# Three weight blocks of the second mixer's compressed columns, cut as two halves of 336 columns

## The chip, the core and the metric

The kernel runs on one core of a Trainium2 chip. The metric is the device time of one launch in microseconds (us), lower is better. Three runs of the kernel before gave 1083.59, 1084.34 and 1084.42 us; their median is 1084.34 us.

## The reference, cut to what matters

The reference applies two transformer-like blocks to one sequence of 256 tokens with 1024 features, in float32. The change touches only the beginning of the second block, where the normalised input is multiplied by the first weight matrix, and there only the columns of the compressed query, the compressed key/value and the shared rotary part: 384 + 256 + 32 = 672 columns.

```
h = rms_norm(x, g_norm)                     # x: 256 tokens x 1024
proj = h @ w_in                             # among others 384 + 256 + 32 columns:
... c_q, c_kv, k_rope ...
q  = rms_norm(c_q, g_cq) @ w_uq             # 384 -> 768
kv = rms_norm(c_kv, g_ckv) @ w_ukv          # 256 -> 1024
k  = concatenate([k_nope, broadcast(k_rope)])
```

## The kernel before, in words

**Precision and products.** Every float32 operand of a big product is split into a rounded high part and a remainder, the low part. One product of two tiles is three matmuls: high by high, high by low, low by high (`product`, lines 523 to 527, and `first_half`, lines 530 to 539, which does the same for the first tile of a block and can make its first matmuls a few columns wider, by the table `WIDER`).

**The weight stream.** All weights come in 171 blocks of 128 x 2048 values (1 MB) in a fixed order (`weight_blocks`, `BLOCKS`, `FIRST`). SyncE loads them into a ring of three raw buffers. ScalarE rounds a block into its high part (`round_block`, line 1373), VectorE subtracts to get the low part (`low_block`, line 2091), and TensorE multiplies. There are three buffers for each of the parts, so ScalarE may round block b + 3 only when TensorE has finished block b: it waits for the counter `block_done`. `after(b)` on ScalarE and `low_after(b)` on VectorE mean "round, or lower, all blocks up to b + 3 that are not done yet". Their places in each engine's program are written out by hand, and every engine works through its program strictly in order, so an instruction behind `after(b)` cannot start before block b is finished on TensorE.

**PSUM banks.** Results go to eight banks. `claim` makes TensorE wait until the last user of a bank has read it (`bank_read`). Blocks usually take bank b modulo 3; the transposes of x take banks 3 to 6.

**The stage of the change.** After the last feed-forward part x is complete. TensorE first transposes raw x (`raw_turn(5)`); ScalarE and VectorE turn that into `sec_hi` and `sec_lo`, which are x times the gain, without the root of the norm. With tokens as the stationary side, three blocks (stages `cq`, `ckv`, `cq_rope`) are then multiplied: 256 columns, 256 columns, and 128 + 32 columns. Each has 2 token tiles x 8 k tiles x 3 = 48 matmuls. Meanwhile VectorE computes the root of the norm and scales x into `sec_xn` (lines 2136 to 2147, semaphore `xn_ready`). Between the second and the third of these blocks TensorE transposes `sec_xn` (`norm_turn(6)`, 16 transposes, line 624); from them ScalarE makes `hT_hi` (`norm_high(6)`, line 1412) and VectorE `hT_lo` (`norm_low(6)`, line 2168), which the next blocks `zz0` to `zz3` use as the moving side. `zz0` waits for its first pair of columns of `hT` only, then for each later pair as it comes to it (`ready=norm_done(6)`).

ScalarE's order here is: wait for `xn_ready` 3, scale `cq0` out of its bank (line 1892), `after` the first block, scale `ckv` out, `after` the second block, `norm_high(6)`, scale `cq1` out, then four sums of squares (lines 1916, 1919), `after` the third block, then the `zz` blocks. VectorE's order is: `norm_low(5)`, weights, sum of squares, root, scale of x (line 2147), weights of the first `zz` block, `norm_low(6)`, weights, then two roots of ten linked steps each for `c_q` and `c_kv` (`inverse_root`, lines 2121 to 2132), four scalings (`c_ready`), weights, and so on. TensorE transposes the scaled `cq` and `ckv` after `zz2` and needs `c_ready` 4 for it.

Of the kernel before, what the change touches and what calls it, by code (L numbers as in the profile page):

```python
# [15 lines left out]
P = 128  # L16
# [53 lines left out]

def weight_blocks():
# [31 lines left out]
    add("cq", "w_in_2", [(W_IN2_AT["cq"], 256)])  # L103
    add("ckv", "w_in_2", [(W_IN2_AT["ckv"], 256)])
    add("cq_rope", "w_in_2", [(W_IN2_AT["cq"] + 256, P), (W_IN2_AT["rope"], QK_ROPE)])
# [55 lines left out]
for _name, _len in [("ssd_dt_bias", 32), ("ssd_A_log", 32), ("ssd_D", 32), ("da_lambda_q1", 64), ("da_lambda_k1", 64),  # L161
# [19 lines left out]
         **dict.fromkeys(("qkv7", "qkv3", "ssd7", "kv3", "kv6", "cq0", "gg2"), (4, 4)),  # L181
         **dict.fromkeys(("gate6", "hy4"), (8, 8)),
         **dict.fromkeys(("xo2", "qkv10", "z3"), (6, 0)),
         "ckv": (4, 0), "qkv9": (2, 0), "qkv8": (12, 0), "z1": (10, 0), "out2": (12, 0)}
# [71 lines left out]
def program(nc, a, out):  # L256
    with ExitStack() as ctx:
# [242 lines left out]
        def _(pe):  # L500
# [639 lines left out]
            at = (0, 1, 2, 7, (FIRST["cq"] + 1) % 3, (FIRST["cq"] + 2) % 3)  # L1140
# [5 lines left out]
            token_block("cq0", FIRST["cq"], 256, sec_hi, sec_lo, ready=norm_done(5))  # L1146
            token_block("ckv", FIRST["ckv"], 256, sec_hi, sec_lo)
            norm_turn(6, sec_xn, 2)
            token_block("cq1", FIRST["cq_rope"], P + QK_ROPE, sec_hi, sec_lo)
            for i in range(4):  # L1150
                feature_block(f"zz{i}", FIRST["z_hy"] + i, 2, hT_hi, hT_lo, ready=None if i else norm_done(6))
                if i == 2:

                    pe.wait_ge(S("c_ready"), 4)
                    for k in range(5):
                        if k % 2 == 0:
                            o = claim(f"cT{k // 2}", 3 + k // 2)
                        for t in range(TOK):
                            src = cq[:, t, k * P:(k + 1) * P] if k < 3 else ckv[:, t, (k - 3) * P:(k - 2) * P]
                            mm = turn(o[:, k % 2 * SEQ + t * P:k % 2 * SEQ + (t + 1) * P], src)  # L1160
                        if k % 2 or k == 4:
                            ends(mm, f"cT{k // 2}")
# [199 lines left out]
        def _(act):  # L1362
# [526 lines left out]
            def token_scale(dst, src):  # L1889

                for t in range(TOK):
                    ins = act.activation(dst[:, t], src[:, t], ACT.Copy, scale=xr[:, t:t + 1])
                return ins

            o = full(act, "cq0")
            act.wait_ge(S("xn_ready"), 3)
            read(token_scale(cq[:, :, 0:256], two(o)), "cq0")
            after(FIRST["cq"])
            o = full(act, "ckv")
            read(token_scale(ckv, two(o)), "ckv")  # L1900
            after(FIRST["ckv"])
            norm_high(6, "g_norm_2", hT_hi)
            act.dma_start(dft_b[:].rearrange("p w s -> p (w s)"), a["c_dft"][:, 1024:1536]).then_inc(S("dft_ab_in"), 16)
            o = full(act, "cq1")
            token_scale(cq[:, :, 256:384], two(o)[:, :, 0:P]).then_inc(S("cq1_in"), 1)
            read(token_scale(k_rope, two(o)[:, :, P:P + QK_ROPE]), "cq1")

            for t in range(TOK):
                if t == 0:

                    wait_read(act, "cq0")
                    wait_read(act, "ckv")
                    act.wait_ge(S("cq1_in"), 1)
                else:
                    act.wait_ge(S("c_ssq"), 2)
# [5 lines left out]
            after(FIRST["cq_rope"])  # L1921
# [148 lines left out]
        def _(dve):  # L2070
# [45 lines left out]
            def inverse_root(dst, sums, n, width, eps, eps_tile=None):  # L2116
# [3 lines left out]
                if eps_tile is None:  # L2120
# [618 lines left out]
            low_after(FIRST["cq"])  # L2739
            norm_low(6, "g_norm_2", hT_hi, hT_lo)  # L2740
            low_after(FIRST["ckv"])
# [3 lines left out]
            inverse_root(rstd[:, 4:6], c_ssq[:, 0, :], 2, Q_LORA, EPS)  # L2745
            inverse_root(rstd[:, 6:8], c_ssq[:, 1, :], 2, KV_LORA, EPS)
# [17 lines left out]
            wait_read(dve, "cq1")  # L2764
# [343 lines left out]
```

## Time and profile before

| | |
|---|---|
| median of three runs | 1084.34 us |
| the profiled execution's own time | 1085.08 us |
| its span, from the first to the last instruction | 1083.2 us |
| TensorE matmul busy | 1075.2 us (99%), 8588 matmuls |
| VectorE busy | 794.2 us (73%) |
| ScalarE busy | 591.9 us (55%) |
| weights and inputs moved by DMA | 190.73 MB, mean 176 GB/s |

Matmuls are pipelined: a row's duration contains the time in flight, so two matmuls that follow each other overlap in the rows. What one costs is read from the distance between the starts of neighbours. PE is TensorE, PEld its weight load, ACT ScalarE, DVE VectorE, SP SyncE. The stage of the change lies between 866 and 885 us of the span.

### The profile page before, as it was taken

How to read it: one execution, taken by the hardware profiler on the slowest of the kernel's cores; microseconds unless marked ns; L12 is line 12 of the kernel's file. 1: busy time of each engine (PE TensorE's matmuls, PEld its weight loads, DVE VectorE, ACT ScalarE, POOL GpSimd, SP SyncE). 2: the span in 40 equal slices, each digit the busy share in tenths (PEclk: the TensorE clock that was granted, in tenths of full speed). 3: DMA queues.
4: the chain of work that ended last, by engine and by line, in shares of the span. 5: the costliest groups of instructions: out<-in, count | busy, mean ns of one | idle time of the engine just before them, and what ended most of it. 6: DMA issues, size and time to landing. Idle time of an engine off the chain costs nothing.

```text
span 1083.2 us, 21122 instructions
## 1 busy us (share of the span) xinstructions
PE 1075.2 (99%) x8588; PEld 1018.8 (94%) x8588; DVE 794.2 (73%) x1117; ACT 591.9 (55%) x842; POOL 0.2 (0%) x4
## 2 busy tenths in 40 slices
PE   9999999999999999999999999999999999999998
PEld 7999999999989999999999998999999799999998
DVE  5665657989999877778778555765655887997784
ACT  5544444578643345878445556444444575655561
POOL 0000000000000000000000000000000000000000
PEclk9999999999999999999999999999999999999999
DMA  9765556455443454444546533465555355543341
GB/s 347 285 221 205 184 182 213 151 203 186 165 156 118 137 194 157 156 160 152 205 167 242 197 109 127 145 231 196 192 182 207 117 177 204 186 156 117 118 155 40
DMA packets 29298, 190.73 MB, mean 176 GB/s; under 512 B 3656, under 2 KB 4521, under 8 KB 7466
## 3 DMA queue, kind: packets, MB, share of 16 engines
q1 hardware_dynamic: 26480, 182.53, 48.4%
q10 hardware_dynamic: 2746, 7.16, 1.9%
q8 instruction: 55, 0.90, 0.3%
q14 instruction: 17, 0.14, 0.0%
HBM read 188.62 MB, written 1.05 MB: 175 GB/s over the span
## 4 chain that ended last, share of the span: by engine, by line
PE 97%; ACT 1%; DVE 1%; DMA 0%; issue 0%; SPq 0%; ACTq 0%; DVEq 0%
PE bank L525 17%; PE bank L526 17%; PE bank L527 17%; PE bank L537 12%; PE bank L538 11%; PE bank L539 11%; PE bank L624 3%; PE bank L760 1%; PE bank L708 1%; PE bank L874 1%; PE bank L1245 1%; PE bank L1037 1%; PE bank L1081 1%; PE bank L1103 1%; PE bank L1210 1%; PE bank L1268 1%
## 5 line engine op out<-in xcount | busy, mean ns | idle before, releaser
L2091 DVE TENSOR_TENSOR sb_w_lo<-sb_w_raw,sb_w_hi 128x2048 fp32r<-128x2048 f32 x169 | 386.5, 2289 | 129.6 <-ACT sb_w_hi L1373 128.9
L1373 ACT ACTIVATE sb_w_hi<-sb_w_raw 128x2048 fp32r<-128x2048 f32 x169 | 322.8, 1910 | 31.4 <-PE bank L527 28.0
L525 PE MATMUL bank<-sb_hT_hi,sb_w_hi 128*128 128x256 f32 (+1 forms) x816 | 225.9, 277 | 0.0
L527 PE MATMUL bank<-sb_hT_hi,sb_w_lo 128*128 128x256 f32 (+1 forms) x816 | 225.9, 277 | 0.0
L526 PE MATMUL bank<-sb_hT_lo,sb_w_hi 128*128 128x256 f32 (+1 forms) x816 | 225.7, 277 | 0.0
L537 PE MATMUL bank<-sb_hT_hi,sb_w_hi 128*128 128x256 f32 (+2 forms) x744 | 213.2, 287 | 0.2 <-DVE sb_hT_lo L2168 0.2
L538 PE MATMUL bank<-sb_hT_lo,sb_w_hi 128*128 128x256 f32 (+2 forms) x744 | 206.3, 277 | 0.0
L539 PE MATMUL bank<-sb_hT_hi,sb_w_lo 128*128 128x256 f32 x744 | 206.1, 277 | 0.0
L526 PEld LDWEIGHTS bank<-sb_hT_lo,sb_w_hi 128*128 128x128 f32 (+1 forms) x816 | 152.8, 187 | 0.0
L527 PEld LDWEIGHTS bank<-sb_hT_hi,sb_w_lo 128*128 128x128 f32 (+1 forms) x816 | 152.7, 187 | 0.0
L525 PEld LDWEIGHTS bank<-sb_hT_hi,sb_w_hi 128*128 128x128 f32 (+1 forms) x816 | 152.6, 187 | 0.0
L537 PEld LDWEIGHTS bank<-sb_hT_hi,sb_w_hi 128*128 128x128 f32 x744 | 140.0, 188 | 3.8 <-issue 2.6
L538 PEld LDWEIGHTS bank<-sb_hT_lo,sb_w_hi 128*128 128x128 f32 x744 | 140.1, 188 | 1.5 <-issue 1.2
L539 PEld LDWEIGHTS bank<-sb_hT_hi,sb_w_lo 128*128 128x128 f32 x744 | 139.9, 188 | 0.0
L1427 ACT ACTIVATE sb_ffn_gate<-sb_ffn_gate 128x256 f32<-128x256 f32 x44 | 18.4, 418 | 133.2 <-DVE sb_ffn_gate L2228 133.2
L525 PE MATMUL bank<-sb_w_hi,sb_ffn_hi 128*128 128x512 f32 x156 | 60.9, 390 | 0.0
L526 PE MATMUL bank<-sb_w_lo,sb_ffn_hi 128*128 128x512 f32 x156 | 60.8, 390 | 0.0
L527 PE MATMUL bank<-sb_w_hi,sb_ffn_lo 128*128 128x512 f32 x156 | 60.8, 390 | 0.0
L1436 ACT ACTIVATE sb_ffn_hi<-sb_ffn_act 128x256 fp32r<-128x256 f32 x44 | 18.3, 416 | 48.0 <-PE bank L760 35.0
L526 PE MATMUL bank<-sb_w_lo,sb_hT_hi 128*128 128x256 f32 (+1 forms) x136 | 39.9, 293 | 0.0
L527 PE MATMUL bank<-sb_w_hi,sb_hT_lo 128*128 128x256 f32 (+1 forms) x136 | 39.9, 293 | 0.0
L525 PE MATMUL bank<-sb_w_hi,sb_hT_hi 128*128 128x256 f32 (+1 forms) x136 | 39.9, 293 | 0.0
(513 smaller groups left out, 2088.0 us busy)
## 6 DMA issues: line engine op xcount, KB each, us to landing
sb_w_raw<-in_w SPq DMA_DIRECT2D x169, 1024.0 KB, 4.9
sb_w_raw<-in_w SPq DMA_DIRECT2D x4, 512.0 KB, 7.6
sb_hT<-in_xT SPq DMA_DIRECT2D x2, 512.0 KB, 5.3
sb_x<-in_x SPq DMA_DIRECT2D x2, 512.0 KB, 11.5
sb_mem_xn<-in_mem ACTq DMA_DIRECT2D x1, 1024.0 KB, 7.3
sb_mem_T<-in_memT ACTq DMA_DIRECT2D x1, 1024.0 KB, 10.6
sb_post_g<-in_ffn_post_g ACTq DMA_DIRECT2D x2, 512.0 KB, 5.7
sb_decay<-in_c_decay ACTq DMA_DIRECT2D x1, 768.0 KB, 5.6
```

The source lines that it names most:

```text
L525: pe.matmul(o, a_hi, b_hi, start=first, stop=False)
L526: pe.matmul(o, a_hi, b_lo, start=False, stop=False)
L527: return pe.matmul(o, a_lo, b_hi, start=False, stop=last)
L537: pe.matmul(o[:, 0:width + more[0]], stat_hi, moving(move_hi, width + more[0]), start=k == 0, stop=False)
L538: pe.matmul(o[:, 0:width + more[1]], stat_hi, moving(move_lo, width + more[1]), start=False, stop=False)
L539: return pe.matmul(o[:, 0:width], stat_lo, moving(move_hi, width), start=False, stop=k == kt - 1)
L624: return pe.transpose(o, src, ident)
L708: mm = pe.matmul(o[:, i * SEQ:(i + 1) * SEQ], w[:, k, i * P:(i + 1) * P], hT[:, k, :], start=False, stop=k == KD - 1 and i == 1)
L1373: act.activation(w_hi[b % STAGES][:], w_raw[b % RING][:], ACT.Copy).then_inc(w_hi_in, 1)
L1427: act.activation(f["gate"][:, j % 2, :], f["gate"][:, j % 2, :], ACT.Silu).then_inc(S("ffn_gate"), 1)
L1436: act.activation(f["hi"][:, j % 2, :], f["act"][:, j % 2, :], ACT.Copy).then_inc(S("ffn_hi"), 1)
L2091: tt(w_lo[b % STAGES][:], w_raw[b % RING][:], f32(w_hi[b % STAGES][:]), ALU.subtract).then_inc(w_lo_in, 1)
```

## The change

The three blocks now hold two halves of 336 columns each, one after the other. Half 0 is the columns 0 to 335 of the compressed query, half 1 its last 48 columns, the 256 of the key/value and the 32 rotary ones. The first block holds the k tiles 0 to 5 of half 0; the second the k tiles 6 and 7 of half 0 and 0 to 3 of half 1; the third the k tiles 4 to 7 of half 1. A matmul is 336 columns wide, and there are 2 x 2 x 8 x 3 = 96 of them in place of 144. Each half and token tile has a bank of its own: the first two count as full when the second block is done, the other two when the third is.

The transposes `norm_turn(6)` stand inside the second block, behind the first token tile of half 1. `zz0` takes bank 6 in place of bank b modulo 3; bank 6 is also the one from which the last pair of `norm_low(6)` is read. On ScalarE `after` the first and `after` the second block come first, then `norm_high(6)`, then the four banks are scaled out. On VectorE the two roots are one of eleven linked steps over four values. The extra widths of `cq0` and `ckv` are gone.

```diff
@@ -66,6 +66,10 @@

 W_IN2_AT = {"hy": 0, "z_hy": 1536, "cq": 2048, "ckv": 2432, "rope": 2688, "z_at": 2720, "gate": 3232}
+
+
+C_WIDTH = Q_LORA + KV_LORA + QK_ROPE
+C_PARTS = (((0, 0, 6),), ((0, 6, 2), (1, 0, 4)), ((1, 4, 4),))


 def weight_blocks():
@@ -100,9 +104,8 @@
     plain("xa_q", "xa_w_q", 0, 4)
     plain("xa_o", "xa_w_o", 0, 4)
     ffn(2)
-    add("cq", "w_in_2", [(W_IN2_AT["cq"], 256)])
-    add("ckv", "w_in_2", [(W_IN2_AT["ckv"], 256)])
-    add("cq_rope", "w_in_2", [(W_IN2_AT["cq"] + 256, P), (W_IN2_AT["rope"], QK_ROPE)])
+    for part in C_PARTS:
+        add("c", "w_in_2", part)
     plain("z_hy", "w_in_2", W_IN2_AT["z_hy"], 2)
     plain("z_at", "w_in_2", W_IN2_AT["z_at"], 2)
     add("uq", "w_uq_2", [(0, 512)], 3)
@@ -178,10 +181,10 @@

 WIDER = {**dict.fromkeys(("xbc1", "xbc10", "xbc11", "qkv1", "gate0", "gate2", "gate3", "gate4", "ssd5", "attn3.0", "zz3", "gg6",
                           "gg7", "hyo1.0", "qkv2", "qkv4", "qkv5", "hy0", "gg0", "gg3", "zz1"), (2, 2)),
-         **dict.fromkeys(("qkv7", "qkv3", "ssd7", "kv3", "kv6", "cq0", "gg2"), (4, 4)),
+         **dict.fromkeys(("qkv7", "qkv3", "ssd7", "kv3", "kv6", "gg2"), (4, 4)),
          **dict.fromkeys(("gate6", "hy4"), (8, 8)),
          **dict.fromkeys(("xo2", "qkv10", "z3"), (6, 0)),
-         "ckv": (4, 0), "qkv9": (2, 0), "qkv8": (12, 0), "z1": (10, 0), "out2": (12, 0)}
+         "qkv9": (2, 0), "qkv8": (12, 0), "z1": (10, 0), "out2": (12, 0)}

@@ -1137,18 +1140,42 @@
             for i in (6, 7):
                 filter_taps(i, (up + 2) % 3 if i == 6 else (up + 1) % 3)
             ffn_part(2, 4)
-            at = (0, 1, 2, 7, (FIRST["cq"] + 1) % 3, (FIRST["cq"] + 2) % 3)
+            at = (0, 1, 2, 7, (FIRST["c"] + 1) % 3, (FIRST["c"] + 2) % 3)
             for i in range(6):
                 filter_spectrum(i, at[i])
             raw_turn(5, x_added(3))
             for i in (6, 7):
                 filter_spectrum(i, at[i - 2])
-            token_block("cq0", FIRST["cq"], 256, sec_hi, sec_lo, ready=norm_done(5))
-            token_block("ckv", FIRST["ckv"], 256, sec_hi, sec_lo)
-            norm_turn(6, sec_xn, 2)
-            token_block("cq1", FIRST["cq_rope"], P + QK_ROPE, sec_hi, sec_lo)
+            c_half, c_ready = C_WIDTH // 2, norm_done(5)
+            c_bank = FIRST["c"] % 3
+
+            def c_block(i):
+
+                hi, lo = weights(FIRST["c"] + i, sum(kt for _, _, kt in C_PARTS[i]), c_half)
+                at = 0
+                for h, first, kt in C_PARTS[i]:
+                    for t in range(TOK):
+                        key = f"c{t}.{h}"
+                        if first == 0:
+                            claim(key, (c_bank, (c_bank + 1) % 3, 7, (c_bank + 2) % 3)[2 * h + t], FIRST["c"] + h + 1)
+                        o = banks[fills[key][0]]
+                        for kk in range(kt):
+                            k = first + kk
+                            if t == 0 and h == 0:
+                                c_ready(k)
+                            a = slice(t * P, (t + 1) * P)
+                            mm = product(o[:, 0:c_half], sec_hi[:, k, a], sec_lo[:, k, a], hi[:, at + kk, :], lo[:, at + kk, :],
+                                         k == 0, k == KD - 1)
+                        if i == 1 and h == 1 and t == 0:
+                            norm_turn(6, sec_xn, 2)
+                    at += kt
+                mm.then_inc(block_done, 1)
+
+            for i in range(3):
+                c_block(i)
             for i in range(4):
-                feature_block(f"zz{i}", FIRST["z_hy"] + i, 2, hT_hi, hT_lo, ready=None if i else norm_done(6))
+                feature_block(f"zz{i}", FIRST["z_hy"] + i, 2, hT_hi, hT_lo, bank=None if i else 6,
+                              ready=None if i else norm_done(6))
                 if i == 2:

                     pe.wait_ge(S("c_ready"), 4)
@@ -1886,31 +1913,29 @@
             act.dma_start(dft_a[:].rearrange("p w f -> p (w f)"), a["c_dft"][:, 0:512]).then_inc(S("dft_ab_in"), 16)
             act.dma_start(m_ropeT[:], a["c_rope"]).then_inc(S("rope_in"), 16)

-            def token_scale(dst, src):
-
-                for t in range(TOK):
-                    ins = act.activation(dst[:, t], src[:, t], ACT.Copy, scale=xr[:, t:t + 1])
-                return ins
-
-            o = full(act, "cq0")
             act.wait_ge(S("xn_ready"), 3)
-            read(token_scale(cq[:, :, 0:256], two(o)), "cq0")
-            after(FIRST["cq"])
-            o = full(act, "ckv")
-            read(token_scale(ckv, two(o)), "ckv")
-            after(FIRST["ckv"])
+            mid = C_WIDTH // 2
+            after(FIRST["c"])
+            after(FIRST["c"] + 1)
             norm_high(6, "g_norm_2", hT_hi)
+            for t in range(TOK):
+                o = full(act, f"c{t}.0")
+                read(act.activation(cq[:, t, 0:mid], o[:, 0:mid], ACT.Copy, scale=xr[:, t:t + 1]), f"c{t}.0")
             act.dma_start(dft_b[:].rearrange("p w s -> p (w s)"), a["c_dft"][:, 1024:1536]).then_inc(S("dft_ab_in"), 16)
-            o = full(act, "cq1")
-            token_scale(cq[:, :, 256:384], two(o)[:, :, 0:P]).then_inc(S("cq1_in"), 1)
-            read(token_scale(k_rope, two(o)[:, :, P:P + QK_ROPE]), "cq1")
+            for t in range(TOK):
+                r = xr[:, t:t + 1]
+                o = full(act, f"c{t}.1")
+                n = Q_LORA - mid
+                act.activation(cq[:, t, mid:], o[:, 0:n], ACT.Copy, scale=r).then_inc(S("c_in"), 1)
+                act.activation(ckv[:, t], o[:, n:n + KV_LORA], ACT.Copy, scale=r).then_inc(S("c_in"), 1)
+                read(act.activation(k_rope[:, t], o[:, n + KV_LORA:mid], ACT.Copy, scale=r), f"c{t}.1")

             for t in range(TOK):
                 if t == 0:

-                    wait_read(act, "cq0")
-                    wait_read(act, "ckv")
-                    act.wait_ge(S("cq1_in"), 1)
+                    wait_read(act, "c0.0")
+                    wait_read(act, "c1.0")
+                    act.wait_ge(S("c_in"), 4)
                 else:
                     act.wait_ge(S("c_ssq"), 2)
                 act.activation(c_junk[:, 0:Q_LORA], cq[:, t, :], ACT.Square, accum_out=c_ssq[:, 0, t:t + 1])\
@@ -1918,7 +1943,7 @@
                 act.wait_ge(S("c_ssq"), 2 * t + 1)
                 act.activation(c_junk[:, 0:KV_LORA], ckv[:, t, :], ACT.Square, accum_out=c_ssq[:, 1, t:t + 1])\
                     .then_inc(S("c_ssq"), 1)
-            after(FIRST["cq_rope"])
+            after(FIRST["c"] + 2)
             for i in range(4):
                 o = full(act, f"zz{i}")
                 read(act.activation((z_hy if i < 2 else z_at)[:, 2 * (i % 2):2 * (i % 2) + 2, :], two(o), ACT.Silu), f"zz{i}")
@@ -2117,7 +2142,11 @@


                 v, h, q = (newton[:, i, 0:n] for i in range(3))
-                if eps_tile is None:
+                if isinstance(width, tuple):
+                    m = n // len(width)
+                    for i, w in enumerate(width):
+                        link(ts(v[:, i * m:(i + 1) * m], sums[:, i * m:(i + 1) * m], 1.0 / w, eps, ALU.mult, ALU.add))
+                elif eps_tile is None:
                     link(ts(v, sums, 1.0 / width, eps, ALU.mult, ALU.add))
                 else:
                     link(stt(v, sums, 1.0 / width, eps_tile, ALU.mult, ALU.add))
@@ -2736,14 +2765,13 @@
             row_squares(x, sec_xn)
             row_root(5, xr[:])
             row_scale(x, sec_xn, xr)
-            low_after(FIRST["cq"])
+            low_after(FIRST["c"])
             norm_low(6, "g_norm_2", hT_hi, hT_lo)
-            low_after(FIRST["ckv"])
+            low_after(FIRST["c"] + 1)


             dve.wait_ge(S("c_ssq"), 4)
-            inverse_root(rstd[:, 4:6], c_ssq[:, 0, :], 2, Q_LORA, EPS)
-            inverse_root(rstd[:, 6:8], c_ssq[:, 1, :], 2, KV_LORA, EPS)
+            inverse_root(rstd[:, 4:8], c_ssq[:].rearrange("p w t -> p (w t)"), 4, (Q_LORA, KV_LORA), EPS)
             for t in range(TOK):
                 ts(cq[:, t, :], cq[:, t, :], rstd[:, 4 + t:5 + t], None, ALU.mult).then_inc(S("c_ready"), 1)
                 ts(ckv[:, t, :], ckv[:, t, :], rstd[:, 6 + t:7 + t], None, ALU.mult).then_inc(S("c_ready"), 1)
@@ -2761,7 +2789,8 @@
                 ins = stt(lo, o[:, k % 2 * SEQ:(k % 2 + 1) * SEQ], g, f32(hi), ALU.mult, ALU.subtract)
                 if k % 2 or k == 4:
                     read(ins, f"cT{k // 2}")
-            wait_read(dve, "cq1")
+            for t in range(TOK):
+                wait_read(dve, f"c{t}.1")
             for t in range(TOK):
                 ins = dve.tensor_copy(mq[:, 1, t, :, QK_NOPE:],
                                       k_rope[:, t, :].unsqueeze(1).to_broadcast([P, MLA_HEADS, QK_ROPE]))
@@ -3071,7 +3100,15 @@


     stream = np.zeros((NBLOCK, P, BLOCK), np.float32)
-    for n, (_, w, first, kt, columns) in enumerate(BLOCKS):
+    for n, (stage, w, first, kt, columns) in enumerate(BLOCKS):
+        if stage == "c":
+            at = 0
+            for half, k, kt in columns:
+                c = W_IN2_AT["cq"] + half * C_WIDTH // 2
+                rows = given[w][0][k * P:(k + kt) * P, c:c + C_WIDTH // 2].reshape(kt, P, -1).transpose(1, 0, 2)
+                stream[n, :, at:at + kt * C_WIDTH // 2] = rows.reshape(P, -1)
+                at += kt * C_WIDTH // 2
+            continue
         rows = given[w][0][first:first + kt * P].reshape(kt, P, -1).transpose(1, 0, 2)
         width = sum(c for _, c in columns)
         part = stream[n, :, 0:kt * width].reshape(P, kt, width)
```

## Rows read from the trace of the kernel before

**Rows 1.** The page: busy time of TensorE, and its granted clock in forty slices.
```profile
PE 1075.2 (99%) x8588; PEld 1018.8 (94%) x8588; DVE 794.2 (73%) x1117; ACT 591.9 (55%) x842; POOL 0.2 (0%) x4
...
PEclk9999999999999999999999999999999999999999
```

**Rows 2.** The page: the chain that ended last, by engine.
```profile
PE 97%; ACT 1%; DVE 1%; DMA 0%; issue 0%; SPq 0%; ACTq 0%; DVEq 0%
```

**Rows 3.** Waits of TensorE: who waited, for whom, total us, times, longest.
```profile
PE bank L624 <- ACT sb_kfil L1397: 1.8, 1, 1.8
...
PE bank L525 <- issue: 0.4, 1, 0.4
```

**Rows 4.** Timeline of TensorE, 866 to 890: start us, us, engine, line, operands, count.
```profile
865.99 0.68 PE L537 MATMUL bank<-sb_w_hi,sb_sec_hi 128*128 128x260 f32 x1
866.51 0.28 PE L538 MATMUL bank<-sb_w_lo,sb_sec_hi 128*128 128x260 f32 x1
...
877.58 0.28 PE L527 MATMUL bank<-sb_w_hi,sb_sec_lo 128*128 128x256 f32 x1
877.70 1.91 PE L624 MATMUL bank<-sb_square,sb_sec_xn 128*128 128x128 f32 x16
879.37 0.32 PE L537 MATMUL bank<-sb_w_hi,sb_sec_hi 128*128 128x160 f32 x1
879.52 0.27 PE L538 MATMUL bank<-sb_w_lo,sb_sec_hi 128*128 128x160 f32 x1
...
884.77 0.32 PE L537 MATMUL bank<-sb_hT_hi,sb_w_hi 128*128 128x256 f32 x1
884.93 0.28 PE L538 MATMUL bank<-sb_hT_lo,sb_w_hi 128*128 128x256 f32 x1
...
890.25 0.28 PE L537 MATMUL bank<-sb_hT_hi,sb_w_hi 128*128 128x258 f32 x1
```

**Rows 5.** Timeline of TensorE in the first feed-forward part.
```profile
180.58 0.39 PE L760 MATMUL bank<-sb_w_hi,sb_ffn_lo 128*128 128x384 f32 x2
180.81 0.33 PE L537 MATMUL bank<-sb_hT_hi,sb_w_hi 128*128 128x256 f32 x1
```

**Rows 6.** Timeline of VectorE: the scaling of x, and the low part of its transposes.
```profile
875.74 1.42 DVE L2147 TENSOR_SCALAR sb_sec_xn<-sb_x,sb_xr 128x1024 f32<-128x1024 f32 x2
...
882.52 3.23 DVE L2168 SCALAR_TENSOR_TENSOR sb_hT_lo<-bank,sb_cols,sb_hT_hi 128x256 fp32r<-128x256 f32 x8 [0.97 <-ACT sb_hT_hi L1412]
```

**Rows 7.** Timeline of ScalarE, 876 to 882.
```profile
876.59 0.84 ACT L1892 ACTIVATE sb_cq<-bank,sb_xr 128x256 f32<-128x256 f32 x2 [5.64 <-DVE sb_sec_xn L2147]
877.32 1.91 ACT L1373 ACTIVATE sb_w_hi<-sb_w_raw 128x2048 fp32r<-128x2048 f32 x1
...
879.83 1.93 ACT L1373 ACTIVATE sb_w_hi<-sb_w_raw 128x2048 fp32r<-128x2048 f32 x1
881.63 3.05 ACT L1412 ACTIVATE sb_hT_hi<-bank,sb_cols 128x256 fp32r<-128x256 f32 x8
```

**Rows 8.** Timeline of VectorE behind the stage.
```profile
888.23 0.17 DVE L2121 TENSOR_SCALAR sb_newton<-sb_c_ssq 128x2 f32<-128x2 f32 x1 [0.28 <-ACT sb_c_junk L1919]
...
893.38 4.49 DVE L2091 TENSOR_TENSOR sb_w_lo<-sb_w_raw,sb_w_hi 128x2048 fp32r<-128x2048 f32 x2
...
907.50 0.87 DVE L2761 SCALAR_TENSOR_TENSOR sb_ckv_lo<-bank,sb_cols,sb_ckv_hi 128x256 fp32r<-128x256 f32 x2
```

**Rows 9.** Timeline of TensorE behind the stage.
```profile
895.73 0.38 PE L537 MATMUL bank<-sb_hT_hi,sb_w_hi 128*128 128x256 f32 x1
...
901.48 0.82 PE L624 MATMUL bank<-sb_square,sb_cq 128*128 128x128 f32 x6
...
908.58 0.47 PE L525 MATMUL bank<-sb_w_hi,sb_cq_hi 128*128 128x512 f32 x1 [0.38 <-issue]
```

**Rows 10.** Timeline of TensorE: 512-wide float32 matmuls at the start, and before the stage.
```profile
3.33 1.92 PE L700 MATMUL bank<-sb_zeros 128*128 128x512 f32 x2
...
860.88 1.98 PE L1037 MATMUL bank<-sb_kfil,sb_dft_f 128*128 128x512 f32 x4
```

## The prediction

> **What bounds the kernel now.** I read the page first. TensorE is busy 1075.2 of 1083.2 us, and its granted clock is 90% or more in all forty slices [rows 1]; the chain that ended last is 97% TensorE [rows 2]. The reader is to see that nothing else can be the bound for the kernel as a whole. Then the waits of TensorE: one of 1.8 us ahead of the transposes of x in another stage, one of 0.4 us ahead of L525, and little else [rows 3]. So the span is the sum of the distances between matmul starts, and a wait newly given to TensorE is paid in full: it has no slack anywhere, while VectorE and ScalarE have. Two things count, then: what the 96 wide matmuls cost against the 144 narrow ones, and whether TensorE still finds what it needs when it gets there. For that I read the timelines of TensorE, VectorE and ScalarE side by side over the stage.
>
> **The products.** The stage runs from 865.99 to 884.77 [rows 4], 18.78 us. After the slow first one, 95 matmuls of 256 columns start from 866.51 to 877.70: 11.19 us, 117.8 ns each. The 160-wide ones start from 879.52 to 884.77: 47 in 5.25 us, 111.7 ns each [rows 4]. The narrow ones thus cost nearly what the wide ones do. Before: 96 x 0.1178 + 48 x 0.1117 = 16.67 us. After: 96 of 336 columns, a width that no row has. From below: a 384-wide and a 128-wide matmul together take 180.81 - 180.58 = 0.23 us for 512 columns [rows 5], which is 0.148 us for 336 if it scales with width. From above: 117.8 x 336 / 256 = 0.155 us, the worst rate of the stage. I take 0.151, between the two because the first is read from wide matmuls and the second from this stage: 14.50 us. The products alone gain 2.17 us (1.8 to 2.4). The total of columns is the same, 32256; what is saved is the cost that does not go with the columns.
>
> Here a rule can be weighed. The Trainium skill, TensorE: Matmul & The Clock Gate, section Back-to-back issue gap, gives for an isolated warm matmul N/2.4 + 2.5 ns. By it 160, 256 and 336 columns cost 69, 109 and 142.5 ns, and the products would go from 13.8 to 13.7 us: no gain at all. The trace disagrees at 160 columns (111.7 ns), so I go by the rows. As it turns out below, neither would change the end of the stage by much.
>
> **The first new wait: the transposes.** They need both halves of the scaled x. VectorE scales x from 875.74 to 877.16 [rows 6]; before, TensorE came to the transposes only at 877.70 [rows 4], 0.5 us later. Nothing in VectorE's program ahead of this is changed, and none of it waits for the products of this stage, so 877.16 stays. After, the transposes stand behind 36 products of the first block, 12 of the rest of half 0 and 12 of half 1: 60 products, and TensorE is there at 866.51 + 59 x 0.151 = 875.42. It waits until 877.24 (877.16 and some 0.08 for the semaphore), 1.8 us. Behind the waiting instruction stand the 12 products of the second token tile, and with them the count that the second block is done. The 16 transposes take 879.37 - 877.70 = 1.67 us as before, until about 878.95 with a slow start.
>
> **The second new wait: ScalarE behind the second block.** ScalarE now stands at `after` the second block before it may touch the transposes. That block ends with its last 12 products: the twelfth starts at 878.95 + 0.04 + 11 x 0.151 = 880.65 and lands 0.3 us later, 880.96. Before, the same rounding began at 879.83, behind the scaling of `ckv`, and the block had been done at about 877.9 [rows 4, 7]. The rounding holds ScalarE 881.63 - 879.83 = 1.80 us [rows 7]; so `norm_high(6)` begins at 881.00 + 1.80 = 882.80, against 881.63. Taking the two scalings of `cq0` and `ckv` out of ScalarE's way (0.84 us twice, [rows 7] for one) gains nothing here, because ScalarE waits for TensorE now. VectorE follows: its eight steps ended 882.52 + 3.23 = 885.75 [rows 6], 4.12 us after `norm_high(6)` began [rows 7], so they end at 886.92.
>
> **The third: bank 6.** Before, `zz0` started at 884.77, 0.98 us before the last of these steps ended, because it asks for each pair of columns by itself [rows 4, 6]. Now it claims bank 6, which the last of the steps reads, so it starts only behind all of them. The way from a VectorE step to such a claim is seen where `uq0` waits: the steps ended at 907.50 + 0.87 = 908.37 [rows 8], the matmul started at 908.58 [rows 9], 0.2 us. So `zz0` starts at 886.92 + 0.2 = 887.1. TensorE has finished the third block at 880.80 + 24 x 0.151 = 884.4 and waits 2.7 us. The sum: 887.1 - 884.77 = 2.3 us later than before, and 0.1 us for the slow second matmul after an idle stretch (0.16 us in place of 0.11 at 884.77 without one, [rows 4]; 0.2 behind a wait, at 895.73, where the next starts at 895.94). That is +2.4 us. The products' own gain of 2.17 us is gone in the two waits (1.8 + 2.7 = 4.5, and 4.5 - 2.17 = 2.3). Note that the time per product enters only through the 12 last ones of the second block: at 0.148 or 0.155 it moves the result by 0.05 us.
>
> **What the rest costs.** `zz0` to `zz3` have 48 matmuls each at (890.25 - 884.93) / 47 = 113.2 ns [rows 4]; other blocks run at 117.8 ns with the same columns, and which of the two a block takes seems to be set by how it starts. `zz0` has a new start, and `zz1` and `zz2` may inherit: each may lose or win 48 x 4.6 ns = 0.22 us. I bound this by -0.3 and +0.45 and take zero. `zz2` stood at 895.73 for its weights for about 0.1 us [rows 9]; that goes, since VectorE has more room by then. Eleven steps of the root in place of twenty save some 1.8 us of VectorE (20 steps from 888.23 to about 892.2, [rows 8]), but the scaled `cq` is needed only at 901.48 [rows 9], and was there before 893.38 [rows 8]. With the four banks scaled behind `norm_high(6)`, the squares end some 2.3 us later than before, the shorter root gives most of it back, and `c_ready` comes at about 893.9, ten us ahead of its use, now 903.8. The weights of `zz2`, lowered next (2.3 us, half of 4.49 [rows 8]), are there at 896.2 and wanted at 898.1. From `zz1` on each engine is released by TensorE as before, so the 0.4 us at `uq0` stay. The DMA issue of `dft_b` is moved by some 6 us and is used fifty us later; the weight loads are bound to the lowered blocks and have landed more than a microsecond ahead of their rounding. Nothing later can give the 2.4 us back, as TensorE has no slack [rows 1, 3].
>
> The profiled execution took 1085.08 us, with a span of 1083.2; its span becomes 1085.6 and its time 1087.5. It lies 0.74 us above the median of the runs, so the median goes from 1084.34 to 1084.34 + 2.4 = 1086.7 us. The likeliest case's own range is 1086.1 to 1087.3: latencies 0.2 each way, the two speeds of a block 0.4.
>
> **The rivals.** A: The gain is real and nothing waits. If `sec_xn` and `hT` were in time, the stage would shorten by the 2.17 us of the products: 1082.2 us. For it speaks only that products and columns add up; against it, VectorE's 877.16 [rows 6] lies 1.7 us behind TensorE's arrival. It would need VectorE to come earlier by that much, and the change moves nothing there.
> B: Only the first wait binds. If `zz0` did not have to wait for bank 6 and could run ahead of `norm_low(6)`, it would start when the first pair is lowered, some 1.8 us behind 882.80, at 884.5, and TensorE is there at 884.4: 0.3 us earlier than before, 1084.1 us. This decides if the claim is passed early; the read of the last pair stands against it.
> C: A further wait behind. ScalarE has its four scalings, squares and a rounding between 885.7 and 892.2 now; if the weights of `zz1` or `zz2` came 1 us late through it, or if ScalarE came late to `zz0`, the time would be 1087.8. The margins of 1.9 us or more above speak against it.
> D: The clock. The transposes' wait and `zz0`'s are 1.8 and 2.7 us of idle TensorE within 12 us. If the clock fell after the second, matmuls would take twice the time, as the 512-wide ones at the start (two in 1.92 us) against those at 860.88 (four in 1.98) [rows 10]. All of `zz0` at half speed is 48 x 0.113 = 5.4 us more: 1092.1. Against it: the idle 1.8 us [rows 3] left the granted clock at 90% or more [rows 1].
> The Trainium skill, TensorE: Matmul & The Clock Gate, section The HAM clock gate, says that an idle stretch takes the clock to half until it has been busy again. No stretch of this trace shows it after the start.
>
> **How the numbers follow.** My forecast has 0.70, A 0.09, B 0.08, C 0.10, D 0.03. What a measurement of this kernel can tell from no change is about 0.2%, 2.17 us, that is 1082.17 and 1086.51. The forecast lies just above that bound, with the likeliest case's spread about three quarters above it: 0.70 x 0.75 = 0.52 slower and 0.18 the same. With C and D slower, B the same, and A just about at the bound and called faster: slower 0.64, same 0.27, faster 0.09. The range leaves out A, D and most of B: 1084.5 to 1087.8.
>
> **What would show it.** Right: the transposes start within 0.2 us of the end of L2147 and behind a TensorE wait of 1.6 to 2 us; `norm_high(6)` begins 1.8 us behind a rounding that was released by the end of the second block; `zz0` starts behind the last step of `norm_low(6)`, after 2.3 to 2.9 us of idle; the 336-wide matmuls stand 0.148 to 0.155 us apart; everything from `zz1` on is shifted by a constant. Wrong: if `zz0` starts before the last step of `norm_low(6)`, if `sec_xn` is ready before 876, or if a further wait appears ahead of `uq0`.

## The result, and the profile after

| | kernel before | kernel after |
|---|---|---|
| median of 11 runs each | 1084.12 us | 1087.40 us |
| lowest and highest | 1083.34 and 1084.98 us | 1085.96 and 1088.60 us |
| ratio, 95% interval | | 1.0030 (1.0023 to 1.0037) |
| the profiled execution, and its span | 1085.08, 1083.2 us | 1085.96, 1084.1 us |

The kernel is slower by 3.3 us, which is more than the 0.2% that can be told from no change. The profiled execution of the kernel after happened to be its fastest of the eleven. Its page shows 48 matmuls fewer and 4.5 us less of busy TensorE, and yet a longer span [rows 1]:

```profile
PE 1070.7 (99%) x8540; PEld 1013.9 (94%) x8540; DVE 792.6 (73%) x1108; ACT 591.9 (55%) x842; POOL 0.2 (0%) x4
...
PEclk9999999999999999999999999999999999999999
```

Where the time went is in the waits of TensorE (who waited, for whom, us, times, longest). In the stage two are new against [rows 3]: the first line, L540 on `hT_lo`, nearly all of it at `zz0`, and the fourth, L627 on `sec_xn`, at the transposes of x:

```profile
PE bank L540 <- DVE sb_hT_lo L2197: 2.6, 2, 2.4
PE bank L627 <- ACT sb_kfil L1424: 1.8, 1, 1.8
PE bank L632 <- DVE sb_zeros L2397: 1.5, 1, 1.5
PE bank L627 <- DVE sb_sec_xn L2176: 1.4, 1, 1.4
PE bank L528 <- DVE sb_ffn_lo L2267: 1.2, 1, 1.2
PE bank L711 <- DMA sb_w_raw<-in_w: 1.1, 1, 1.1
PE bank L540 <- DVE sb_w_lo L2124: 0.5, 1, 0.5
PE bank L528 <- issue: 0.4, 1, 0.4
```

The others lie outside the stage. Two of them, 1.2 us on `sb_ffn_lo` and 0.5 us on `sb_w_lo`, are not in the list of the kernel before either; they stand in the first 27 us of the span, in unchanged code, and differ from profile to profile of the same kernel. At the transposes at 672 us both profiles are level again (672.64 before, 672.62 after), so they explain nothing here. The timeline of TensorE shows both new waits in place; columns as in [rows 4], and the brackets hold the idle time before the row:

```profile
865.43 0.72 PE L528 MATMUL bank<-sb_w_hi,sb_sec_hi 128*128 128x336 f32 x1
865.98 0.31 PE L529 MATMUL bank<-sb_w_lo,sb_sec_hi 128*128 128x336 f32 x1
...
874.94 0.32 PE L530 MATMUL bank<-sb_w_hi,sb_sec_lo 128*128 128x336 f32 x1
876.66 1.97 PE L627 MATMUL bank<-sb_square,sb_sec_xn 128*128 128x128 f32 x16 [1.40 <-DVE sb_sec_xn L2176]
878.38 0.40 PE L528 MATMUL bank<-sb_w_hi,sb_sec_hi 128*128 128x336 f32 x1
...
883.85 0.32 PE L530 MATMUL bank<-sb_w_hi,sb_sec_lo 128*128 128x336 f32 x1
886.56 0.36 PE L540 MATMUL bank<-sb_hT_hi,sb_w_hi 128*128 128x256 f32 x1 [2.40 <-DVE sb_hT_lo L2197]
886.76 0.28 PE L541 MATMUL bank<-sb_hT_lo,sb_w_hi 128*128 128x256 f32 x1
...
910.12 0.47 PE L528 MATMUL bank<-sb_w_hi,sb_cq_hi 128*128 128x512 f32 x1 [0.37 <-issue]
```

The 60th matmul of the stage starts at 874.94 and costs 0.15 us, so TensorE is free at 875.09; the transposes start at 876.66. Counted from the stage's start TensorE is there after 9.66 us, in place of 11.71 before. Of these 2.05 us, 12 x 0.1545 = 1.85 us come from the new place of the transposes, 12 matmuls further forward, and only 0.2 us from cheaper products. The 96th starts at 883.85, `zz0` at 886.56. And what TensorE waits for, from the timelines of ScalarE and of VectorE, the rows that answer to [rows 6, 7]:

```profile
875.97 1.91 ACT L1400 ACTIVATE sb_w_hi<-sb_w_raw 128x2048 fp32r<-128x2048 f32 x1 [5.58 <-DVE sb_sec_xn L2176]
880.57 1.92 ACT L1400 ACTIVATE sb_w_hi<-sb_w_raw 128x2048 fp32r<-128x2048 f32 x1 [2.68 <-PE bank L530]
...
882.38 3.02 ACT L1439 ACTIVATE sb_hT_hi<-bank,sb_cols 128x256 fp32r<-128x256 f32 x8
```

```profile
875.18 1.42 DVE L2176 TENSOR_SCALAR sb_sec_xn<-sb_x,sb_xr 128x1024 f32<-128x1024 f32 x2
...
883.24 3.22 DVE L2197 SCALAR_TENSOR_TENSOR sb_hT_lo<-bank,sb_cols,sb_hT_hi 128x256 fp32r<-128x256 f32 x8 [3.03 <-ACT sb_hT_hi L1439]
```

ScalarE's second rounding stands behind 2.68 us of idling that TensorE ends: it waits for the second block, while the transposes that it needs next have been there since 878.6. VectorE idles 3.03 us behind ScalarE, and TensorE 2.4 us behind VectorE. The second wait is not the first one passed on. From the end of the second block (about 880.31) both ways start together: TensorE needs 3.69 us for the third block, to 884.00, while the rounding, `norm_high(6)`, `norm_low(6)` and the claim end 6.25 us later, at 886.56. The difference, 2.56 us, would be there without the first wait; this is worked out from the rows, as no run has the second wait alone.

Since every profile has its own offset, I read a stage from its own first matmul. Up to it the kernel after was 0.56 us ahead (865.43 against 865.99), where no instruction is changed; to `zz0` it takes 21.13 us in place of 18.78, +2.35; to `uq0` 44.69 in place of 42.59, +2.10; behind `uq0` it needs 0.60 us less, again in unchanged code. The sum is +0.9, the difference of the two spans. The parts in unchanged code I take as what one execution differs from the next by, and +2.10 as the change.

### The profile page after: what moved, and what is told of

It reads as the page before. It is cut to its first block, busy times and chain, and to the rows that moved or that the text cites. A ratio compares the mean times of both kernels' runs of the same rounds, so it can differ in the third digit from the quotient of the medians.

```text
span 1084.1 us, 21015 instructions
## 1 busy us (share of the span) xinstructions
PE 1070.7 (99%) x8540; PEld 1013.9 (94%) x8540; DVE 792.6 (73%) x1108; ACT 591.9 (55%) x842; POOL 0.2 (0%) x4
## 3 DMA queue, kind: packets, MB, share of 16 engines
q10 hardware_dynamic: 2746, 7.16, 1.9%
## 4 chain that ended last, share of the span: by engine, by line
PE 94%; DVE 2%; ACT 2%; DMA 1%; issue 1%; SPq 0%; ACTq 0%; DVEq 0%
PE bank L528 16%; PE bank L530 16%; PE bank L529 16%; PE bank L540 11%; PE bank L541 11%; PE bank L542 11%; PE bank L627 3%; PE bank L763 1%; DMA sb_w_raw<-in_w 1%; PE bank L877 1%; DVE sb_w_lo L2116 1%; PE bank L711 1%; PE bank L1272 1%; PE bank L1084 1%; PE bank L1106 1%
## 5 line engine op out<-in xcount | busy, mean ns | idle before, releaser
L540 PE MATMUL bank<-sb_hT_hi,sb_w_hi 128*128 128x256 f32 (+2 forms) x744 | 212.9, 286 | 3.1 <-DVE sb_hT_lo L2197 2.6
L540 PEld LDWEIGHTS bank<-sb_hT_hi,sb_w_hi 128*128 128x128 f32 x744 | 139.9, 188 | 7.3 <-issue 6.1
L1454 ACT ACTIVATE sb_ffn_gate<-sb_ffn_gate 128x256 f32<-128x256 f32 x44 | 18.4, 418 | 134.3 <-DVE sb_ffn_gate L2257 134.3
L2431 DVE SCALAR_TENSOR_TENSOR sb_ssd_conv<-bank,sb_cols,sb_ssd_conv 128x255 f32<-128x255 f32 (+2 forms) x72 | 34.7, 482 | 6.9 <-ACT sb_ssd_conv L1631 4.7
```

The source lines that it names most:

```text
L540: pe.matmul(o[:, 0:width + more[0]], stat_hi, moving(move_hi, width + more[0]), start=k == 0, stop=False)
L1454: act.activation(f["gate"][:, j % 2, :], f["gate"][:, j % 2, :], ACT.Silu).then_inc(S("ffn_gate"), 1)
L2431: ins = stt(v[:, j:SEQ], u[:, 0:SEQ - j], col("ssd_conv_w", taps * ch + taps - 1 - j), v[:, j:SEQ], ALU.mult, ALU.add)
```

## The experiments

**The kernel after, once more.** The 2.1 us of the trace don't make up 3.3 us of the medians. So the first run is the changed kernel itself, once more, with a second profile.

> The changed kernel once more, for its granted clock run by run. Theory 1 (idle TensorE lets its clock fall): the runs fall in two groups, those at clock 1.000 near 1086.2 us and those at 0.998 near 1087.5 us, and in a profiled run at 0.998 the matmuls right behind the wait for bank 6 stand twice as far apart for a while. Rival (the spread comes from elsewhere, the weight loads for instance): no such pairing of clock and time, and the matmuls behind the wait keep their 113 ns.

Measured: 1087.78 us (7 runs, 1087.05 to 1088.19) against 1084.30, ratio 1.0030 (1.0018 to 1.0041). The span is 1086.2 us, and its mean granted clock is 0.998 where the first profile has 1.000. The page can't show where, because each of its forty slices is 27 us; the windows view can (window: us, then busy time of PE, PEld, DVE, ACT, POOL, then granted clock, DMA share, GB/s):

```profile
884.00:886.60 2.60, 0.23 (x2) 0.00 (x0) 2.60 (x8) 2.60 (x8) 0.00 (x0) 1.00 0.44 176
886.60:887.87 1.27, 1.24 (x11) 1.27 (x12) 1.27 (x1) 1.27 (x6) 0.00 (x0) 1.00 0.00 0
887.87:891.28 3.41, 3.41 (x19) 3.41 (x18) 1.86 (x7) 3.32 (x9) 0.00 (x0) 0.50 0.41 98
891.28:899.00 7.72, 7.72 (x69) 7.72 (x69) 6.59 (x11) 2.99 (x3) 0.00 (x0) 1.00 0.50 173
```

The timeline of TensorE around it:

```profile
886.63 0.36 PE L540 MATMUL bank<-sb_hT_hi,sb_w_hi 128*128 128x256 f32 x1 [2.40 <-DVE sb_hT_lo L2197]
...
887.75 0.30 PE L540 MATMUL bank<-sb_hT_hi,sb_w_hi 128*128 128x256 f32 x1
887.87 0.40 PE L541 MATMUL bank<-sb_hT_lo,sb_w_hi 128*128 128x256 f32 x1
888.07 0.41 PE L542 MATMUL bank<-sb_hT_hi,sb_w_lo 128*128 128x256 f32 x1
888.28 0.42 PE L540 MATMUL bank<-sb_hT_hi,sb_w_hi 128*128 128x256 f32 x1
...
893.79 0.28 PE L540 MATMUL bank<-sb_hT_hi,sb_w_hi 128*128 128x258 f32 x1
```

The stage is the same to 0.01 us up to `zz0` (865.49 to 886.63, 21.14 us). Then, 1.2 us into `zz0`, the granted clock falls from its upper level (2.4 GHz) to the lower (1.2 GHz) for 3.41 us, the distance of two matmuls goes from 0.12 to 0.21 us, and `zz1` starts 7.16 us behind `zz0`, where it takes 5.54 us in the first profile (886.56 to 892.10): 1.62 us more. All seven runs have 0.998, so the two groups that were expected don't show in this set. They show in the eleven timings of the first comparison: three runs at 1.000 have 1085.96, 1086.25 and 1086.30 us, the eight at 0.998 have 1086.63 to 1088.60 with a median of 1087.6. Of all 24 executions of kernels whose profile has the 2.4 us wait at `zz0` (these two sets and the last experiment below), 20 show 0.998; all 50 of the kernel before whose clock is on record show 1.000.

**Another bank for `zz0`.** Bank 3 is the first one that `norm_low(6)` leaves. With it `zz0` no longer waits for the last step.

```diff
-                feature_block(f"zz{i}", FIRST["z_hy"] + i, 2, hT_hi, hT_lo, bank=None if i else 6,
+                feature_block(f"zz{i}", FIRST["z_hy"] + i, 2, hT_hi, hT_lo, bank=None if i else 3,
```

> zz0 claims bank 3, read first by norm_low(6), in place of bank 6, read last. Theory (the claim of bank 6 is the third wait): zz0 starts behind the first pair, about 884.4, in place of 886.6, and is then held by the last pair until 886.5, so the two token halves end about 1.5 to 2.2 us earlier; the idle stretch shrinks from 2.4 us to about 0.5 and the granted clock is 1.000 in every run: 1084.3 us (2 us below the undisturbed runs of the changed kernel, 3 below its median). Rival (zz0 is held by the columns of hT anyway, the bank is no matter): zz0 still starts near 886.5, 1087.4 us.

Measured: 1084.12 us (11 runs), ratio 1.0000 (0.9991 to 1.0009), clock 1.000 in all. The timelines of TensorE and of VectorE:

```profile
883.09 0.32 PE L530 MATMUL bank<-sb_w_hi,sb_sec_lo 128*128 128x336 f32 x1
883.50 0.36 PE L540 MATMUL bank<-sb_hT_hi,sb_w_hi 128*128 128x256 f32 x1
```

```profile
882.48 3.23 DVE L2197 SCALAR_TENSOR_TENSOR sb_hT_lo<-bank,sb_cols,sb_hT_hi 128x256 fp32r<-128x256 f32 x8 [3.03 <-ACT sb_hT_hi L1439]
```

`zz0` starts at 883.50, 18.83 us behind the stage's start, in place of 21.13; `norm_low(6)` still runs from 882.48 to 885.71. The whole loss is gone while ScalarE and VectorE are as late as in the kernel after: it hung on the claim. No gain appears: the first wait is still there, `zz0` waits 0.26 us for its first pair of columns (883.50 - 883.09 - 0.15), and beside `norm_low(6)` it takes 5.78 us to `zz1` where the kernel after takes 5.54.

**The idle time filled.** If idling is what the clock answers to, work in the gap must make the kernel faster. 22 matmuls of 160 columns go into columns of a bank that nothing uses; what they compute is used nowhere.

```diff
+                if i == 2:
+                    for _ in range(22):
+                        mm = pe.matmul(banks[(c_bank + 2) % 3][:, 336:496], sec_hi[:, 7, 0:P], hi[:, 3, 0:160],
+                                       start=True, stop=True)
                 mm.then_inc(block_done, 1)
```

> The changed kernel with 22 matmuls of 160 columns added behind the third block, into unused columns of a bank, about 2.4 us of TensorE work that fills the wait for bank 6 and computes nothing that is used. Theory 1 (the idle stretch lets the clock fall): granted clock 1.000 in every run, and the median falls from 1087.4 to about 1086.2 us although work is added. Rival (the clock does not matter, or falls for another reason): the median stays at 1087.4 or rises with the added work.

Measured: 1086.24 us (11 runs, 1085.89 to 1086.81), ratio 1.0016 (1.0007 to 1.0025), clock 1.000 in all eleven. On the same chip that is 1.5 us below the changed kernel without them. The timeline of TensorE:

```profile
884.22 2.58 PE L1174 MATMUL bank<-sb_w_hi,sb_sec_hi 128*128 128x160 f32 x22
886.78 0.36 PE L540 MATMUL bank<-sb_hT_hi,sb_w_hi 128*128 128x256 f32 x1
```

`zz0` starts 21.14 us behind the stage's start and `uq0` 44.69, to 0.01 us as in the first profile. The first new wait stands as it was (1.40 us), the second is as long as before but filled. So the fall of the clock is the only thing taken away, and it is worth about 1.5 us of the median; 1086.24 - 1084.30 = 1.9 us is what the waits cost by themselves.

**The transposes behind the whole second block, and bank 3.** This keeps the two halves and undoes where the transposes stand.

```diff
-                        if i == 1 and h == 1 and t == 0:
-                            norm_turn(6, sec_xn, 2)
                     at += kt
                 mm.then_inc(block_done, 1)
+                if i == 1:
+                    norm_turn(6, sec_xn, 2)
```

> The halves stay, but the transposes stand behind the whole second block, as they did before, and zz0 claims bank 3. Theory (the products gain 16.67 - 14.83 = 1.8 us and only the waits took it): TensorE reaches the transposes 0.1 us or less ahead of the scaled x, ScalarE is released at 877.3, norm_high(6) begins near 880.3, and zz0 starts at about 882.4 without a wait: 1084.1 - 1.8 = 1082.3 us. Rival (the wide matmuls or the new order cost something of their own later): the same time as before, 1084.1 us, or more.

Measured: 1082.17 us (10 runs, 1080.83 to 1083.08), ratio 0.9979 (0.9969 to 0.9988), clock 1.000 in all: 2.1 us faster than the kernel before, the largest gain here. The timeline of TensorE has no bracket left in the stage:

```profile
877.63 1.91 PE L627 MATMUL bank<-sb_square,sb_sec_xn 128*128 128x128 f32 x16
...
883.09 0.29 PE L540 MATMUL bank<-sb_hT_hi,sb_w_hi 128*128 128x256 f32 x1
...
906.57 0.47 PE L528 MATMUL bank<-sb_w_hi,sb_cq_hi 128*128 128x512 f32 x1 [0.38 <-issue]
```

ScalarE rounds two blocks back to back and is at the transposes 14.17 us behind the stage's start, 2.8 us earlier than in the kernel after (16.95), and VectorE idles 0.23 us in place of 3.03:

```profile
876.66 3.72 ACT L1400 ACTIVATE sb_w_hi<-sb_w_raw 128x2048 fp32r<-128x2048 f32 x2 [5.58 <-DVE sb_sec_xn L2176]
...
880.29 3.00 ACT L1439 ACTIVATE sb_hT_hi<-bank,sb_cols 128x256 fp32r<-128x256 f32 x8
```

```profile
881.14 3.23 DVE L2197 SCALAR_TENSOR_TENSOR sb_hT_lo<-bank,sb_cols,sb_hT_hi 128x256 fp32r<-128x256 f32 x8 [0.23 <-ACT sb_hT_hi L1439]
```

To `zz0` it takes 883.09 - 866.12 = 16.97 us against 18.78. The gain of the products, 1.8 us, is what the two halves are worth once nothing waits; at `uq0` it is 2.1 us. TensorE comes to the transposes 11.51 us behind the stage's start, 0.2 us earlier than before the change and 0.3 us behind `sec_xn`; I had expected a wait of up to 0.1 us.

**The same with bank 6.** The edit is the one above without the bank (run beside its own 22 runs of the kernel before, median 1083.83).

> As the run with the transposes behind the second block, but zz0 keeps bank 6. Theory (bank 6 costs the distance between TensorE's arrival and the last step of norm_low(6)): that step ended 1.3 us behind TensorE's arrival there, so zz0 starts 1.5 us later: 1082.2 + 1.5 = 1083.7 us, granted clock 1.000. Rival (bank 6 costs only together with the late ScalarE): 1082.2 us.

Measured: 1082.61 us (11 runs), ratio 0.9989 (0.9980 to 0.9998). `zz0` starts 18.34 us behind the stage's start, 1.4 us later than with bank 3. The row is a lesson in reading (timeline of TensorE, then of VectorE):

```profile
882.75 0.32 PE L530 MATMUL bank<-sb_w_hi,sb_sec_lo 128*128 128x336 f32 x1
884.28 0.36 PE L540 MATMUL bank<-sb_hT_hi,sb_w_hi 128*128 128x256 f32 x1 [1.22 <-issue]
```

```profile
880.95 3.23 DVE L2197 SCALAR_TENSOR_TENSOR sb_hT_lo<-bank,sb_cols,sb_hT_hi 128x256 fp32r<-128x256 f32 x8 [0.23 <-ACT sb_hT_hi L1439]
```

The bracket names no releaser, but 880.95 + 3.23 = 884.18 is 0.10 us ahead of 884.28, the same 0.10 us as in the kernel after (883.24 + 3.22 = 886.46, then 886.56). It is the claim of bank 6. So this bank costs 1.4 us even without the first wait. The clock was 1.000 in all runs: 1.2 us of idling was not followed by a fall. My forecast of 1083.7 us was 1.1 us too high; 0.5 us of that is the lower median of the kernel before beside these runs (1083.83 against 1084.30), the rest, 0.6 us, is less than the spread of either set of runs. The interval overlaps that of the version with bank 3, so the medians alone don't tell the two apart.

**Only ScalarE's order.** Everything is as in the kernel after, but ScalarE makes `hT_hi` ahead of the rounding that waits for the second block.

```diff
             after(FIRST["c"])
-            after(FIRST["c"] + 1)
             norm_high(6, "g_norm_2", hT_hi)
+            after(FIRST["c"] + 1)
```

> The changed kernel with one edit: ScalarE does norm_high(6) before it waits for the second block and rounds the next weights; bank 6 and the place of the transposes stay. Theory (the rounding behind the second block is what makes norm_low(6) late): norm_high(6) begins near 878 in place of 882.4, norm_low(6) is done near 883.5, before TensorE has finished the third block at 884, and zz0 does not wait: 1086.2 - 2.5 = 1083.7 us, clock 1.000. The 1.4 us wait for the scaled x stays. Rival (bank 6 alone is the wait, whatever ScalarE does): zz0 still idles by 2 us or more, 1086 us or more.

Measured: 1083.28 us (11 runs, against 1083.83 before), ratio 0.9995 (0.9986 to 1.0005), no difference from the kernel before that can be told, clock 1.000 in all. The timelines of ScalarE, VectorE and TensorE:

```profile
877.80 3.01 ACT L1439 ACTIVATE sb_hT_hi<-bank,sb_cols 128x256 fp32r<-128x256 f32 x8
```

```profile
880.13 3.22 DVE L2197 SCALAR_TENSOR_TENSOR sb_hT_lo<-bank,sb_cols,sb_hT_hi 128x256 fp32r<-128x256 f32 x8
```

```profile
883.87 0.31 PE L530 MATMUL bank<-sb_w_hi,sb_sec_lo 128*128 128x336 f32 x1
884.03 0.28 PE L540 MATMUL bank<-sb_hT_hi,sb_w_hi 128*128 128x256 f32 x1
```

`norm_high(6)` starts 12.35 us behind the stage's start, in place of 16.95, and the last low part is there at 883.35, before TensorE has done the third block. `zz0` keeps bank 6 and doesn't wait. So in the kernel after the bank costs only because ScalarE is late, and ScalarE is late because of the one line. What remains of the loss is the first wait, 1.4 us by the bracket and 1.57 us by the starts, which eats most of the products' 1.8 us: `zz0` comes 18.58 us behind the stage's start, 0.2 ahead of the kernel before.

**Two roots again.** The last part of the change, undone alone:

```diff
-            inverse_root(rstd[:, 4:8], c_ssq[:].rearrange("p w t -> p (w t)"), 4, (Q_LORA, KV_LORA), EPS)
+            inverse_root(rstd[:, 4:6], c_ssq[:, 0, :], 2, Q_LORA, EPS)
+            inverse_root(rstd[:, 6:8], c_ssq[:, 1, :], 2, KV_LORA, EPS)
```

> The changed kernel with the two roots of ten steps each restored in place of the one of eleven. Theory (the shorter root is off the path): within 0.3 us of the changed kernel's 1087.4 us; VectorE is 1.8 us later at c_ready, which is still eight us ahead of its use. Rival (the shorter root does part of the work of keeping the weights of zz2 in time): a new wait ahead of zz2 of up to 1 us, 1088.4 us.

Measured: 1087.89 us (6 runs, against 1083.83 before), ratio 1.0035 (1.0023 to 1.0047); five of the runs had a clock of 0.998 and 1087.64 to 1088.23 us, one had 1.000 and 1085.51 us. The profile has the two waits and the slow stretch, with `zz0` 21.14 us behind the stage's start (timeline of TensorE):

```profile
886.22 0.41 PE L540 MATMUL bank<-sb_hT_hi,sb_w_hi 128*128 128x256 f32 x1 [2.40 <-DVE sb_hT_lo L2197]
886.43 0.42 PE L541 MATMUL bank<-sb_hT_lo,sb_w_hi 128*128 128x256 f32 x1
```

Here the clock falls 0.15 us into `zz0`, not 1.2 us, and again for 3.4 us; `zz1` comes 7.13 us behind `zz0`, 1.6 us late. VectorE's chain is longer by 1.8 us with two roots, and `c_ready` still comes nine us ahead of its use. The shorter root is worth nothing that these runs can tell.

## Why the prediction was right

**The direction and the two waits.** The forecast was 1086.7 us with slower at 0.64; the median is 1087.40, inside the range of 1084.5 to 1087.8. The mechanism, two new waits that take back more than the products save, is what the runs show. That the number lies in the range is in part luck: the waits cost 0.3 us less than forecast, and a fall of the clock that the forecast had left out cost over a microsecond more. Point by point, all in us from the stage's first matmul (865.99 in the prediction's count, 865.43 in the profile after):

| step | forecast | measured |
|---|---|---|
| transposes of x start | 11.25 | 11.23 |
| ScalarE's rounding behind the second block | 15.01 | 15.14 |
| `norm_high(6)` starts | 16.81 | 16.95 |
| `norm_low(6)` ends | 20.93 | 21.03 |
| TensorE through with the third block | 18.4 | 18.6 |
| `zz0` starts | 21.1 | 21.13 |
| `uq0` starts, against before | +2.4 | +2.10 |

The chain of reasons is shown, and not only argued: with ScalarE's order put right the second wait is gone, with another bank it is all but gone too, and with the transposes further back and bank 3 both are gone and a gain of the products of 1.8 us appears. With the transposes further back alone the first wait is gone and 1.4 us of the second stay.

Of the signs that the prediction named, the first wait misses its band: 1.57 us by the starts (1.40 by the bracket) against 1.6 to 2, because the wider matmuls bring TensorE there 0.2 us later than forecast. The way from `sec_xn` to the transposes, for which the sum had 0.08 us from no row, is 0.06 us here (876.66 - 876.60). The idle time at `zz0`, the distance of the 336-wide matmuls and the order of events are as it said. From `zz1` on the shift is not quite a constant: it is +2.41 us at `zz1` and +2.10 at `uq0`. And the load of `dft_b` is issued 1.8 us later within the stage, not 6, which costs nothing either way.

**The cost of a 336-wide matmul.** It was taken as 0.151 us, with 0.155 as the upper bound. Measured: (874.94 - 865.98) / 58 = 0.1545. The reading from 384 and 128 columns together [rows 5] was too low, the one from the worst rate of the stage right. The products' gain is thus 16.67 - 96 x 0.1545 = 1.84 us, not 2.17. As the working said, it hardly enters the result: 12 x 0.0035 = 0.04 us through the second block. It would have been a miss of a third of a microsecond had nothing waited, as the version with the transposes further back shows (1.8 us at `zz0`).

**The way from VectorE to the claim.** 0.2 us was taken from `uq0`; it is 0.10 us here. The idle time of TensorE at `zz0` is then 886.56 - (883.85 + 0.15) = 2.56 us against 2.7.

**Behind `zz0`.** Forecast were +0.1 us for the slow start and nothing else. From `zz0` to `uq0` the kernel after is 0.25 us shorter (910.12 - 886.56 = 23.56 against 23.81): `zz2` doesn't wait for its weights, for which the prediction had 0.1 us that it named but left out of the sum, and it runs at 0.113 us a matmul in place of 0.118. This lies within the -0.3 to +0.45 that it gave.

**The clock: the step that was mis-sized.** Case D had a chance of 0.03, and its price was all of `zz0` at half speed, 5.4 us. The runs show a mean clock below 1.000 in 20 of 24 executions; in the two profiles that have it the fall lasts 3.41 us and not the whole block, at a price of 1.6 us, and between the runs with and without it lie 1.4 us. The forecast of the waits (+2.4) and the median without it (1086.25 - 1084.12 = +2.1) agree to 0.3 us; the median with it is +3.3. The argument against D was that a wait of 1.8 us left the clock alone [rows 1, 3]. That was true, and it said nothing on 2.4 us so soon behind another 1.4 us. What the Trainium skill, TensorE: Matmul & The Clock Gate, says for D in its section The HAM clock gate, that an idle stretch takes the clock to half, was set aside on one row. The Trainium skill, TensorE: Matmul & The Clock Gate, section HAM oscillation — how this bites in real kernels, tells of a kernel that waits between groups of matmuls and starts the next group at the lower clock. This case's traces agree in part: the clock falls behind the wait, but 1.2 us into the group in one profile and 0.15 us in the other.

**The other cases.** A (nothing waits, 1082.2) is what the kernel becomes when the transposes stand further back and `zz0` takes bank 3: 1082.17. B (only the first wait binds, 1084.1) is what it becomes with bank 3 (1084.12) or with ScalarE's order alone (1083.28). C didn't happen.

**What stays open.** Why the clock falls in most executions and not in all with the same waits, and why at different places: the first profile has the same two brackets, 1.40 and 2.40 us, as the second, and no fall. Whether the 2.4 us alone would do it, without the 1.4 us ten microseconds before, wasn't tried. Why blocks of the same width run at 0.113 or 0.118 us a matmul, and change between executions, is open too; a block of 48 changes by 0.2 us with it, as `zz2` does here.

## What to carry to other kernels

On an engine that is 99% busy, saving instructions is worth only what its feeders can keep up with: before products are shortened, ask of each operand behind them whether it was early by more than the saving (here `sec_xn` was early by 0.5 us), and of each instruction moved forward whether its operand comes forward too: TensorE came to the transposes 2.05 us earlier, 1.85 us of it because they had been moved. In a program that runs strictly in order, work on data that is already there belongs ahead of a wait for the end of a block; moving one line on ScalarE was worth 2.6 us at `zz0`. Idling on TensorE can cost more than it lasts, here 2.4 us of it another 1.4 to 1.6 us in most executions. So a profile's mean clock of 0.998 is to be looked into, and the idle time to be removed or, where it can't be, filled.

## What the runs showed of the hardware

A gap of 2.4 us on TensorE, ten microseconds behind one of 1.4 us, was followed in 20 of 24 executions by a mean granted clock below 1.000, in the two profiles that have it by 3.4 us at the lower level. In none of the 11 executions with the gap filled was it, nor in any of the kernels with one gap of 1.4 us or of 1.2 us in the stage, or of 1.8 us elsewhere. Adding 22 matmuls that compute nothing of use made the kernel 1.5 us faster. A matmul of 336 columns costs 0.1545 us, of 256 columns 0.113 or 0.118, of 160 columns 0.112 us: between 160 and 256 columns the width hardly changes the cost.
